# Three gate evictions moved between attention units, and the sink made the initial value of the maximum

## The chip, the cores and the metric

The kernel runs on one core of one Trainium2 chip, as one launch. The metric is the device time of the launch in microseconds (us). The kernel before takes 884.95 us, the median of three runs (884.6 to 885.35). A profiled execution is a run of its own with its own time, so every sum is made against that one and then set beside the median.

## The reference, cut to what matters

Two transformer blocks run over 256 tokens of width 1024, all in float32. The first block has two layers. Its second layer has two attention parts and a gate for each: part c (three branches: selected keys, window keys and 15 compressed keys) with gate z_c, and part d (a window of 128 keys with a learned sink for each head) with gate z_d.

```
def _masked_softmax(s, mask, sink=None):
    s = jnp.where(mask, s, NEG)
    m = jnp.max(s, axis=-1, keepdims=True)
    if sink is not None:
        m = jnp.maximum(m, sink)
    e = jnp.where(mask, jnp.exp(s - m), 0.0)
    den = jnp.sum(e, axis=-1, keepdims=True)
    if sink is not None:
        den = den + jnp.exp(sink - m)
    return e / jnp.maximum(den, TINY)

y_c = _merge_heads(o_c) * jax.nn.silu(z_c)
y_d = _merge_heads(o_d) * jax.nn.silu(z_d)
x = x + concat(y_c, y_d) @ w_out[layer]
```

So for part d the maximum takes the sink in, and the denominator gets exp(sink - maximum) added. d_sinks is one number for each of 8 heads.

## The kernel before, in words

The five engines run five instruction lists written out by hand, and semaphores order them; there is no planner. Nearly all matrix products are split in three (high by high, low by high, high by low), so TensorE has most of the work. ScalarE makes the high parts of the weights, GpSimd the low parts; both also serve other work.

**The stage of the change.** The attention of the second layer is the call `narrow_attention(PART["c"] + PART["d"], FILL_CD)`: 16 units. Units 0 to 11 are part c: for each pair of heads (0, 1) and each half of the queries (0, 1) three branches, where the branches with real keys have 128 or 256 key columns and the third has 15. Units 12 to 15 are part d. A unit holds four heads and passes through these steps:

- `scores(u)` on TensorE, eight small matmuls into two PSUM banks;
- `score_max(u)` on VectorE: scale, bias and maximum. For c with real keys and for d it is four fused operations (L1983, in the trace CUSTOM_DVE_ANT_0 with a DVE_READ_ACCUMULATOR2_ANT behind each) and a short reduction that negates;
- `exps(u)` on ScalarE: four Exp with the negated maximum as bias and the sum as accumulator (L1507);
- `normalise(u)` on VectorE: reciprocal, gate factor, and one wide multiplication (L2043);
- `transposes(u, r)` on TensorE (L990), then `transposed_out(u)` on ScalarE (L1540);
- `mix(step)` on TensorE (L1021) once the last unit of a step is there, and `mixed_out` on VectorE (L2060), which frees the bank for the next mix.

**What is put between.** `FILL_CD` has one list of names for each unit i. TensorE does, at unit i: scores(i+2), transposes(i), the mix of unit i-1 if it ended a step, then the names of the list. A name such as `zc1.0` is half of the product of gate z_c, heads 1 (24 matmuls), `zd0.0.0` a quarter (12). `H:0` and `H:1` are the first quarters of the output product, and they read parts of y whose low half GpSimd makes (L711) from a high half that ScalarE makes (`L:y0`, `L:y1`, L1634).

A name `E:zc1` is the eviction of a gate. It is skipped by TensorE and has two halves. ScalarE does a tanh of the bank (L1550), at unit i ahead of exps(i+1). VectorE then does (tanh + 1) times the bank (L2071) and frees the bank; at unit i this stands behind normalise(i) and ahead of mixed_out and of score_max(i+2). Each engine takes its list in order, so what waits holds all that stands behind it.

**Banks.** Two PSUM banks serve the products of this stage in turn: bank 0 holds zc0, zc1, zd0 and wo1_0 one after the other, bank 1 holds sp_kd, modA, zd1 and wo1_1. So the first matmul of zc1.0 waits for the eviction of zc0, that of zd0.0.0 waits for that of zc1, and H:0 (wo1_0 and wo1_1) waits for those of zd0 and zd1.

**Scaled biases.** Part d needs its bias table scaled; `scale_bias("d", pair, half)` on ScalarE is four copies (L1524), and the dictionaries SCALE_BEFORE and SCALE_BEHIND say at which unit it stands ahead of or behind transposed_out. (0, 0) stands behind transposed_out(2) before the change. The first reader is score_max(12).

**The sink before.** `score_max` of a d unit reduces to `top` in PSUM (L2008), takes the minimum with the negated sinks `no_sinks` (L2014), copies it to the statistics (L2016) and adds the sinks (L2017). ScalarE makes one Exp over the four sums (L1510). `no_sinks` is made once at the start (L2191).

Of the kernel before, what the change touches and what calls it, by code (L numbers as in the profile page):

```python
# [7 lines left out]
ALU = mybir.AluOpType  # L8
ACT = mybir.ActivationFunctionType
AX = mybir.AxisListType  # L10
# [53 lines left out]
    "S: N:kd E:zc0", "zc1.0 E:kd", "zc1.1", "E:zc1", "modA zd0.0.0", "zd0.0.1 E:modA", "",  # L64
    "zd0.1", "zd1.0 E:zd0", "", "zd1.1.0", "zd1.1.1", "L:y0", "H:0 E:zd1 L:y1", "H:1", "")]
SCALE_BEFORE, SCALE_BEHIND = {6: (0, 1), 12: (1, 1)}, {2: (0, 0), 7: (1, 0)}
# [249 lines left out]
def mixer_kernel(nc, a, out):  # L316
    ctx = ExitStack()
    with ctx:
# [14 lines left out]
        def cut(ap, n):  # L333
            return ap.rearrange("p (k n) -> p k n", n=n)
# [57 lines left out]
        stream_rstd, no_sinks = rstd[:, 352:356], rstd[:, 360:368]  # L392
# [165 lines left out]
        def root_of(name):  # L558

            return q_rms[:, "cd".index(name[1]), int(name[2])] if name[0] == "q" else rstd_of(name)  # L560

# [850 lines left out]
        def _(act):  # L1412
# [85 lines left out]
            def exps(u):  # L1498
                part, step, br, last_br, at, qt, n = UNITS[u]
                act.wait_ge(mx_ready, u + 1)  # L1500
                s, e = stat[:, u % 3], prob(u)
                if part == "a":
                    nc.scalar.activation(e[:, 0:AG, 0:n], e[:, 0:AG, 0:n], ACT.Exp, bias=s[:, 4:5],
                                         accum_out=s[:, 8:9]).then_inc(exp_done, 1)
                    return
                for i in range(4):
                    last = nc.scalar.activation(e[:, i, 0:n], e[:, i, 0:n], ACT.Exp, bias=s[:, 4 + i:5 + i],  # L1507
                                                accum_out=s[:, 8 + i:9 + i])
                if part == "d":
                    last = nc.scalar.activation(s[:, 12:16], s[:, 12:16], ACT.Exp)  # L1510
                last.then_inc(exp_done, 1)
# [355 lines left out]
        def _(dve):  # L1867
# [92 lines left out]
            def score_max(u):  # L1960
# [17 lines left out]
                if part == "d" or part == "c" and br:  # L1978
                    dve.wait_ge(sem(f"{part}_bias"), 2 * at + qt + 1)
                    for i in range(4):  # L1980
                        f, bi = divmod(i, 2)
                        i8 = 4 * qt + 2 * bi + f
                        ins = V.tensor_tensor_reduce(out=e[:, i, 0:n], in0=sc[f][:, S * bi:S * bi + n], in1=bias_of(part, at, qt, i),  # L1983
                                                     scale=q_rstd[:, "bcd".index(part), at, i8:i8 + 1], scalar=-3e38,
                                                     op0=ALU.add, op1=ALU.max, accum_out=s[:, 8 + i:9 + i])
                    ins.then_inc(sc_free, 1)
                    dve.wait_ge(sc_free, u + 1)
                    if part == "c":
                        V.tensor_reduce(s[:, 4:8], s[:, 8:12].unsqueeze(2), AX.X, ALU.max, negate=True).then_inc(mx_ready, 1)
                        return  # L1990
# [17 lines left out]
                own.did(V.tensor_reduce(top, e[:, :, 0:n] if part == "c" else s[:, 8:12].unsqueeze(2), AX.X, ALU.max, negate=True))  # L2008
                own.settle()
                if part == "c":  # L2010
                    V.tensor_scalar(s[:, 4:8], top, 1e28, None, ALU.min).then_inc(mx_ready, 1)
                    return
                sk, down = (cut(v[:], 4)[:, :, 2 * at:2 * at + 2] for v in (sinks, no_sinks))
                own.did(V.tensor_tensor(cut(top, 2), cut(top, 2), down, ALU.min))  # L2014
                own.settle()
                own.did(V.tensor_copy(s[:, 4:8], top))  # L2016
                V.tensor_tensor(cut(s[:, 12:16], 2), cut(top, 2), sk, ALU.add).then_inc(mx_ready, 1)  # L2017
# [173 lines left out]
            own.did(V.tensor_scalar(no_sinks, sinks, -1.0, None, ALU.mult))  # L2191
# [475 lines left out]
```

## Time and profile before

| what | value |
|---|---|
| median of the runs shown | 884.95 us (884.6 to 885.35) |
| the profiled execution's own time | 884.18 us |
| its span | 882.4 us |
| TensorE busy | 863.6 us, 98% of the span |
| ScalarE busy | 468.2 us, 53% |
| VectorE busy | 408.9 us, 46% |
| GpSimd busy | 674.2 us, 76% |
| mean granted TensorE clock | 0.996 |
| chain that ended last | TensorE 95%, VectorE 2%, ScalarE 1% |

How to read it: 1.78 us lie around the span in the profiled execution (884.18 less 882.4). A row of the timeline has the start, the length of the merged piece, engine, line and operation, what is written and read, how many instructions, and in brackets the idle time of the engine just before and what released it. An instruction's start can lie ahead of the end of the one before it, since the engines overlap the ends; so the distance between two starts is the price of an instruction in a row of them, and its length that of one that somebody waits for.

### The profile page before, as it was taken

What the parts mean: (1) busy time and instruction counts of PE and PEld (TensorE: products, weight loads), DVE (VectorE), ACT (ScalarE), POOL (GpSimd) and SP (SyncE); (2) the same over time, 40 slices, a digit from 0 to 9 for tenths busy, and PEclk for the clock granted to TensorE, in tenths of its full rate; (3) what the DMA queues carried; (4) which work ended last, traced back from release to release, by engine and by line L of the source; (5) the groups of instructions that cost most, each with busy time, mean ns of one, the idle gap of its engine ahead of it and who ended that gap; (6) DMA issues with size and microseconds to landing.
All of it is one profiled execution on the core that took longest, in us unless ns stands there. A gap on an engine that the chain in (4) does not pass through costs nothing.

```text
span 882.4 us, 17028 instructions
## 1 busy us (share of the span) xinstructions
PE 863.6 (98%) x6944; PEld 817.8 (93%) x6944; DVE 408.9 (46%) x1015; ACT 468.2 (53%) x706; POOL 674.2 (76%) x552
## 2 busy tenths in 40 slices
PE   7999999999989999999999999999999999999997
PEld 6899899998879999889997899999999999999997
DVE  3899745635785576953554223321124642210001
ACT  4545766377876623344444565875336665534431
POOL 0987549748935799798767787678899899987880
PEclk9999999999999999999999999999999999999998
DMA  8855586884210597876575444545546555545521
GB/s 324 339 186 198 204 292 226 307 313 144 87 59 2 205 408 261 344 276 242 195 268 181 166 144 148 188 143 192 191 147 246 191 186 188 189 144 191 192 96 48
DMA packets 28484, 177.62 MB, mean 201 GB/s; under 512 B 3144, under 2 KB 5844, under 8 KB 8056
## 3 DMA queue, kind: packets, MB, share of 16 engines
q1 hardware_dynamic: 27112, 174.87, 54.0%
q10 hardware_dynamic: 1296, 1.68, 0.6%
q8 instruction: 55, 0.90, 0.4%
q14 instruction: 21, 0.17, 0.1%
HBM read 174.95 MB, written 3.43 MB: 202 GB/s over the span
## 4 chain that ended last, share of the span: by engine, by line
PE 95%; DVE 2%; ACT 1%; issue 1%; POOL 1%; DMA 1%; POOLq 0%; SPq 0%; DVEq 0%; ACTq 0%
PE proj L793 20%; PE proj L795 19%; PE proj L796 19%; PE proj L829 4%; PE proj L874 3%; PE proj L872 3%; PE proj L875 3%; PE mixed L1021 1%; PE scores L976 1%; PE transposed L990 1%; PE proj L1074 1%; PE proj L1143 1%; PE mixed L1004 1%; PE scores L963 1%; PE proj L1077 1%; PE proj L1076 1%
## 5 line engine op out<-in xcount | busy, mean ns | idle before, releaser
L695 POOL TENSOR_TENSOR w_lo<-raw,w_hi 128x512 fp32r<-128x512 f32 x348 | 445.2, 1320 | 126.3 <-ACT w_hi L1434 126.3
L795 PE MATMUL proj<-parts,w_lo 128*128 128x256 f32 x1000 | 279.4, 279 | 0.6 <-POOL w_lo L695 0.6
L793 PE MATMUL proj<-parts,w_hi 128*128 128x256 f32 x952 | 270.3, 284 | 0.6 <-POOL w_lo L695 0.4
L796 PE MATMUL proj<-parts,w_hi 128*128 128x256 f32 x952 | 265.8, 279 | 0.0
L1434 ACT ACTIVATE w_hi<-raw 128x2048 fp32r<-128x2048 f32 x84 | 161.0, 1917 | 109.3 <-DMA raw<-in_weights 58.9
L795 PEld LDWEIGHTS proj<-parts,w_lo 128*128 128x128 f32 x1000 | 188.1, 188 | 1.7 <-POOL w_lo L695 0.8
L793 PEld LDWEIGHTS proj<-parts,w_hi 128*128 128x128 f32 x952 | 179.0, 188 | 3.4 <-issue 2.2
L796 PEld LDWEIGHTS proj<-parts,w_hi 128*128 128x128 f32 x952 | 179.0, 188 | 0.0
L695 POOL TENSOR_TENSOR w_lo<-arena,w_hi 128x512 fp32r<-128x512 f32 (+2 forms) x56 | 67.7, 1245 | 27.3 <-ACT w_hi L1434 27.3
L1446 ACT ACTIVATE arena<-proj 128x512 f32<-128x512 f32 x32 | 18.9, 597 | 53.2 <-PE proj L796 36.5
L872 PE MATMUL proj<-w_hi,parts 128*128 128x512 f32 x112 | 45.1, 403 | 0.0
L796 PE MATMUL proj<-hid_lo,w_hi 128*128 128x256 f32 x160 | 44.9, 281 | 0.0
L793 PE MATMUL proj<-hid_hi,w_hi 128*128 128x256 f32 x160 | 44.9, 281 | 0.0
L795 PE MATMUL proj<-hid_hi,w_lo 128*128 128x256 f32 x160 | 44.9, 281 | 0.0
L874 PE MATMUL proj<-w_lo,parts 128*128 128x512 f32 x112 | 44.4, 396 | 0.0
L875 PE MATMUL proj<-w_hi,parts 128*128 128x512 f32 x112 | 44.3, 395 | 0.0
L695 POOL TENSOR_TENSOR w_lo<-raw,w_hi_a 128x512 fp32r<-128x512 f32 x28 | 37.7, 1386 | 4.1 <-ACT w_hi_a L1434 4.1
L2518 DVE SCALAR_TENSOR_TENSOR xT<-proj,mod,xT 128x256 f32<-128x256 f32 x8 | 3.9, 484 | 79.1 <-PE proj L796 79.1
L695 POOL TENSOR_TENSOR w_lo<-raw,w_hi_b 128x512 fp32r<-128x512 f32 x20 | 26.4, 1369 | 9.5 <-ACT w_hi_b L1434 9.4
L2538 DVE SCALAR_TENSOR_TENSOR scores<-proj,tmp 128x512 f32<-128x512 f32 x14 | 9.8, 699 | 44.0 <-ACT tmp L1842 44.0
L793 PEld LDWEIGHTS proj<-hid_hi,w_hi 128*128 128x128 f32 x160 | 30.2, 188 | 0.0
L796 PEld LDWEIGHTS proj<-hid_lo,w_hi 128*128 128x128 f32 x160 | 30.1, 188 | 0.0
(448 smaller groups left out, 2157.0 us busy)
## 6 DMA issues: line engine op xcount, KB each, us to landing
raw<-in_weights SPq DMA_DIRECT2D x106, 1024.0 KB, 5.0
arena<-in_weights SPq DMA_DIRECT2D x31, 1024.0 KB, 7.6
wide<-in_weights SPq DMA_DIRECT2D x9, 1024.0 KB, 6.9
probT<-in_weights SPq DMA_DIRECT2D x8, 1024.0 KB, 5.0
dil_lines<-dil_line SPq DMA_DIRECT2D x1, 2304.0 KB, 12.3
prob<-in_weights SPq DMA_DIRECT2D x2, 1024.0 KB, 4.8
dil_bias<-dil_lines SPq DMA_DIRECT2D x1, 1536.0 KB, 9.8
xT<-in_x SPq DMA_DIRECT2D x4, 256.0 KB, 5.6
```

Source lines behind the costliest of these rows:

```text
L695: nc.gpsimd.tensor_tensor(lo_slots[RAW_AT[n]][:, at], raw_slots[RAW_AT[n]][:, at], hi_slots[HI_AT[m]][:, at].bitcast(F32), ALU.subtract).t ...
L793: nc.tensor.matmul(dst, whi, h, start=first, stop=False)
L795: nc.tensor.matmul(dst, wlo, h, start=False, stop=False)
L796: last = nc.tensor.matmul(dst, whi, lo[:, k, :], start=False, stop=stop)
L829: last = nc.tensor.matmul(pair["banks"][i][:, S * j:S * j + S], w[low][:, k, P * j:P * j + P], parts[:, part, k, :], start=fresh, stop=fin ...
L872: nc.tensor.matmul(banks[t], parts[:, 0, kk, at], whi[:, k, :], start=kk == 0, stop=False)
L874: nc.tensor.matmul(banks[t], parts[:, 0, kk, at], wlo[:, k, :], start=False, stop=False)
L875: last = nc.tensor.matmul(banks[t], parts[:, 1, kk, at], whi[:, k, :], start=False, stop=kk == KD - 1)
L963: last = nc.tensor.matmul(sc[g // 2][:, S * (g % 2):S * (g % 2) + n], q, akT[:, g, S * at:S * at + n], start=True, stop=True)
L1434: nc.scalar.activation(hi_slots[HI_AT[m]][:, 0:kt * w], raw_slots[RAW_AT[n]][:, 0:kt * w], ACT.Copy) \
L1446: nc.scalar.activation(dst, b[:], fn, scale=scale).then_inc(free_of(name), 1)
L2538: V.scalar_tensor_tensor(square, bank(name)[:], 0.0, r, ALU.max, ALU.mult).then_inc(free_of(name), 1)
```

## The change

The evictions of zc0, zc1 and zd1 move to other units: zc0 from unit 0 to 1, zc1 from 3 to 4, zd1 from 13 to 12. The scaled bias (0, 0) moves from behind transposed_out(2) to behind transposed_out(3). In the d units the sink is the `scalar` of the fused operation, that is the value the maximum starts from; the three short operations and the sums behind them go, and ScalarE makes exp(sink - maximum) as four Exp of one column with the sink column as input and the negated maximum as bias, where there was one Exp of four columns. `no_sinks` goes.

```
 FILL_CD = [x.split() for x in (
-    "S: N:kd E:zc0", "zc1.0 E:kd", "zc1.1", "E:zc1", "modA zd0.0.0", "zd0.0.1 E:modA", "",
-    "zd0.1", "zd1.0 E:zd0", "", "zd1.1.0", "zd1.1.1", "L:y0", "H:0 E:zd1 L:y1", "H:1", "")]
-SCALE_BEFORE, SCALE_BEHIND = {6: (0, 1), 12: (1, 1)}, {2: (0, 0), 7: (1, 0)}
+    "S: N:kd", "zc1.0 E:zc0 E:kd", "zc1.1", "", "E:zc1 modA zd0.0.0", "zd0.0.1 E:modA", "",
+    "zd0.1", "zd1.0 E:zd0", "", "zd1.1.0", "zd1.1.1", "E:zd1 L:y0", "H:0 L:y1", "H:1", "")]
+SCALE_BEFORE, SCALE_BEHIND = {6: (0, 1), 12: (1, 1)}, {3: (0, 0), 7: (1, 0)}
...
-        stream_rstd, no_sinks = rstd[:, 352:356], rstd[:, 360:368]
+        stream_rstd = rstd[:, 352:356]
...
+        def sink_of(at, i):
+
+            f, b = divmod(i, 2)
+            return sinks[:, 2 * at + b + 4 * f:][:, 0:1]
...
-                if part == "d":
-                    last = nc.scalar.activation(s[:, 12:16], s[:, 12:16], ACT.Exp)
+                for i in range(4) if part == "d" else ():
+                    last = nc.scalar.activation(s[:, 12 + i:13 + i], sink_of(at, i), ACT.Exp, bias=s[:, 4 + i:5 + i])
...
                         ins = V.tensor_tensor_reduce(out=e[:, i, 0:n], in0=sc[f][:, S * bi:S * bi + n], in1=bias_of(part, at, qt, i),
-                                                     scale=q_rstd[:, "bcd".index(part), at, i8:i8 + 1], scalar=-3e38,
+                                                     scale=q_rstd[:, "bcd".index(part), at, i8:i8 + 1],
+                                                     scalar=sink_of(at, i) if part == "d" else -3e38,
                                                      op0=ALU.add, op1=ALU.max, accum_out=s[:, 8 + i:9 + i])
...
-                    if part == "c":
-                        V.tensor_reduce(s[:, 4:8], s[:, 8:12].unsqueeze(2), AX.X, ALU.max, negate=True).then_inc(mx_ready, 1)
-                        return
+                    V.tensor_reduce(s[:, 4:8], s[:, 8:12].unsqueeze(2), AX.X, ALU.max, negate=True).then_inc(mx_ready, 1)
+                    return
...
-                sk, down = (cut(v[:], 4)[:, :, 2 * at:2 * at + 2] for v in (sinks, no_sinks))
-                own.did(V.tensor_tensor(cut(top, 2), cut(top, 2), down, ALU.min))
-                own.settle()
-                own.did(V.tensor_copy(s[:, 4:8], top))
-                V.tensor_tensor(cut(s[:, 12:16], 2), cut(top, 2), sk, ALU.add).then_inc(mx_ready, 1)
+                V.tensor_scalar(s[:, 4:8], top, 1e28, None, ALU.min).then_inc(mx_ready, 1)
...
-            own.did(V.tensor_scalar(no_sinks, sinks, -1.0, None, ALU.mult))
```

## Rows read from the trace of the kernel before

**Rows 1.** The page: its first line, span and number of instructions.
```profile
span 882.4 us, 17028 instructions
```

**Rows 2.** Busy time by stretch: stretch, length, PE, PEld, DVE, ACT, POOL, clock, DMA, GB/s.
```profile
203.00:272.00 69.00, 64.60 (x639) 56.81 (x637) 49.83 (x220) 51.10 (x181) 50.76 (x54) 1.00 0.21 73
...
874.00:876.00 2.00, 0.83 (x5) 0.75 (x6) 0.27 (x2) 1.08 (x3) 0.00 (x0) 0.95 0.00 0
```

**Rows 3.** Timeline of TensorE, units 0 to 6 of the stage.
```profile
210.26 0.62 PE L976 MATMUL scores<-arena 64*128 64x15 f32 x8
...
213.82 0.37 PE L1074 MATMUL proj<-parts,w_hi 128*128 128x256 f32 x1
...
225.63 0.66 PE L990 MATMUL proj<-cols,wide 128*128 128x128 f32 x4 [0.66 <-DVE wide L2043]
...
226.70 0.36 PE L1074 MATMUL proj<-parts,w_hi 128*128 128x256 f32 x1
...
231.59 0.66 PE L990 MATMUL transposed<-cols,prob 128*128 128x128 f32 x4
```

**Rows 4.** Timeline of VectorE over the same units.
```profile
210.56 0.69 DVE L2071 SCALAR_TENSOR_TENSOR arena<-arena,proj 128x512 f32<-128x512 f32 x1 [1.27 <-ACT arena L1550]
211.17 0.65 DVE L1996 SCALAR_TENSOR_TENSOR prob<-scores,q_rstd,cmp_bias 128x15 f32<-128x15 f32 x4
...
212.67 0.69 DVE L2043 TENSOR_TENSOR wide<-wide,sums 128x512 f32<-128x512 f32 x1
...
221.96 0.69 DVE L2071 SCALAR_TENSOR_TENSOR arena<-arena,proj 128x512 f32<-128x512 f32 x1 [0.51 <-ACT arena L1550]
...
225.49 0.42 DVE L2060 SCALAR_TENSOR_TENSOR arena<-mixed,arena 128x256 f32<-128x256 f32 x1
225.82 0.34 DVE L1983 CUSTOM_DVE_ANT_0 prob<-scores,dil_bias,q_rstd 128x128 f32<-128x128 f32 x1
...
230.85 0.69 DVE L2043 TENSOR_TENSOR prob<-prob,sums 128x512 f32<-128x512 f32 x1
```

**Rows 5.** Timeline of ScalarE, units 2 to 4.
```profile
219.01 1.27 ACT L1524 ACTIVATE dil_bias<-arena,q_rms 128x128 f32<-128x128 f32 x4
221.32 0.60 ACT L1550 ACTIVATE arena<-proj 128x512 f32<-128x512 f32 x1 [1.04 <-PE proj L1077]
...
224.92 0.59 ACT L1540 ACTIVATE probT<-transposed 128x512 f32<-128x512 f32 x1
225.40 0.31 ACT L1507 ACTIVATE prob<-prob,stat 128x15 f32<-128x15 f32 x1
```

**Rows 6.** Timeline of VectorE: end of the maximum of a c unit, then a d unit.
```profile
219.62 0.09 DVE L1983 DVE_READ_ACCUMULATOR2_ANT stat<- 128x1 f32 x1
219.74 0.16 DVE L1989 TENSOR_REDUCE stat<-stat 128x4 f32<-128x4 f32 x1
...
252.57 0.08 DVE L1983 DVE_READ_ACCUMULATOR2_ANT stat<- 128x1 f32 x1
...
253.26 0.15 DVE L2017 TENSOR_TENSOR stat<-sums,cols 128x4 f32<-128x4 f32 x1
```

**Rows 7.** Timeline of ScalarE, unit 12.
```profile
255.44 0.19 ACT L1510 ACTIVATE stat<-stat 128x4 f32<-128x4 f32 x1
255.53 1.70 ACT L1524 ACTIVATE arena<-arena,q_rms 128x256 f32<-128x256 f32 x4
257.79 0.60 ACT L1540 ACTIVATE probT<-transposed 128x512 f32<-128x512 f32 x1 [0.55 <-PE mixed L1021]
```

**Rows 8.** Timeline of TensorE, units 12 and 13.
```profile
254.69 0.66 PE L990 MATMUL transposed<-cols,prob 128*128 128x128 f32 x4 [1.18 <-DVE prob L2043]
...
260.60 0.66 PE L1021 MATMUL mixed<-probT,arena 128*64 128x128 f32 x8 [0.83 <-DVE arena L2060]
261.18 0.38 PE L829 MATMUL proj<-parts,w_hi_b 128*128 128x256 f32 x1
```

**Rows 9.** Timeline of GpSimd, the low part that H:0 reads.
```profile
258.98 1.27 POOL L711 TENSOR_TENSOR parts<-arena,parts 128x512 fp32r<-128x512 f32 x1 [11.43 <-ACT parts L1634]
```

More of the change, by code:

```diff
@@ L2007, in score_max @@
                 top = st[:, S + 12 + 4 * (u % 3):S + 12 + 4 * (u % 3) + 4]
-                own.did(V.tensor_reduce(top, e[:, :, 0:n] if part == "c" else s[:, 8:12].unsqueeze(2), AX.X, ALU.max, negate=True))
+                own.did(V.tensor_reduce(top, e[:, :, 0:n], AX.X, ALU.max, negate=True))
                 own.settle()
-                if part == "c":
-                    V.tensor_scalar(s[:, 4:8], top, 1e28, None, ALU.min).then_inc(mx_ready, 1)
-                    return
-                sk, down = (cut(v[:], 4)[:, :, 2 * at:2 * at + 2] for v in (sinks, no_sinks))
-                own.did(V.tensor_tensor(cut(top, 2), cut(top, 2), down, ALU.min))
-                own.settle()
-                own.did(V.tensor_copy(s[:, 4:8], top))
-                V.tensor_tensor(cut(s[:, 12:16], 2), cut(top, 2), sk, ALU.add).then_inc(mx_ready, 1)
+                V.tensor_scalar(s[:, 4:8], top, 1e28, None, ALU.min).then_inc(mx_ready, 1)
             def normalise(u):
```

## The prediction

> **What bounds the kernel now.** I read the page first: a span of 882.4 us [rows 1], in which TensorE is the engine of nearly the whole chain. A change that adds and takes no TensorE work can then only move the stretches in which TensorE stands still. The second view is the busy time by stretch. In the stage of the change, from 203 to 272 us, TensorE is busy 64.60 of 69.00 us at a granted clock of 1.00, and no other engine is near that [rows 2]. So 4.4 us of standing still is all that is at stake in the stage. The third view is the timeline of each engine through the 16 units; there one looks for the bracket behind a TensorE row. The larger brackets are 0.66 us ahead of transposes(4) [rows 3], 1.18 us ahead of transposes(12) and 0.83 us ahead of the mix of unit 12 [rows 8]. They name VectorE, whose list in turn waits for ScalarE. What TensorE loses or gains here stays to the end, since behind the stage each engine's work starts from TensorE's products again.
>
> **The sink.** Its work is off TensorE, but it lies in the path score, maximum, Exp, normalise, transpose. On VectorE the distance from the start of the last accumulator read to the end of the maximum is 0.84 us in a d unit (252.57 to 253.26 + 0.15) and 0.28 us in a c unit, which already has the new form (219.62 to 219.74 + 0.16) [rows 6]. So each d unit gives back 0.56 us. The pointer as initial value has no row: the fused operation of a c unit has one pointer already. The nearest thing is an accumulator read, 0.08 us [rows 6]; the bounds are 0 and four times that, 0.32 us a unit, and I take 0, as the number of instructions stays. On ScalarE one Exp of four columns becomes four of one column. The one in the trace lasts 0.19 us, but the next starts 0.09 us behind it [rows 7]. Three more cost 3 x 0.09 = 0.27 us if they overlap likewise, 3 x 0.19 = 0.57 us if not. I take 0.27, the row of starts. The net is 0.29 us off the path of each d unit; TensorE sees it only where it waits for it. The negated sinks at the start are one small VectorE operation while TensorE has a first product in hand; nothing.
>
> Here the Trainium skill speaks against the change. ScalarE: Activation LUTs, "Rules for kernel authors", budgets about 0.3 us for every ACTIVATE with a pointer as bias; three more would be an estimate of 0.9 us, more than the 0.56 us saved. The row of starts here disagrees with it for a short operation.
>
> **zc0, from unit 0 to unit 1.** Before, VectorE waited 1.27 us for the tanh, and the eviction then stood ahead of the maximum of unit 2, which started at 211.17 [rows 4]. Its scores were done at 210.26 + 0.62 = 210.88 [rows 3], so it now starts some 0.06 later, 0.23 us earlier than before. Normalise(1) follows it, its wide multiplication at 212.67 - 0.23 = 212.44; the eviction starts 0.61 behind (the distance of the rows at 210.56 and 211.17 is that of one 512-wide operation) at 213.05 and ends at 213.74 [rows 4]. The product zc1.0 must wait for it, and the shortest handover in the rows is 0.05 (wide operation ending at 230.85 + 0.69 = 231.54, transposes at 231.59 [rows 3, 4]); for a product whose weights are loaded behind the wait I estimate 0.1 to 0.15. That is 213.9 against 213.82 [rows 3]: **0.1 us lost** in place of nothing won. The tanh itself is hidden in ScalarE's idle time.
>
> **zc1, from unit 3 to unit 4, with the scaled bias.** This is the large term. ScalarE's list at unit 3 is now exps(4), transposed_out(3), the four copies of the bias, and only then, at unit 4, the tanh of zc1. transposed_out(3) can't come earlier: it waits for TensorE's mix. Its second half starts at 224.92 and what follows at 225.40 [rows 5]. The copies take 1.27 us less the 0.09 of overlap, 1.2 [rows 5, 7]. So the tanh starts at 226.6 and ends at 227.2, with 0.1 us from zc0 at 227.3, where it started at 221.32 before [rows 5]. zd0.0.0 needs the bank of zc1: the eviction takes 0.69 us [rows 4], so it ends at about 228.0 and the product starts at 228.1, not at 226.70 [rows 3]. **Here TensorE stands still for some 1.9 us**, in place of 0.66. It doesn't end there: the eviction holds VectorE's list, in which mixed_out and the maximum of unit 6 stand behind it. From the eviction's start at 227.3 the maximum of unit 6 begins 0.61 + 0.33 later (distances of starts [rows 4]), at 228.2, against 225.82 before: 2.4 us later. From there VectorE has no idle time in the trace up to normalise(6), whose wide operation started at 230.85 and ended at 231.54, and transposes(6) start at 231.59 [rows 3, 4]. All of that moves by the 2.4. So the cost is **2.4 us** from transposes(6) on (1.4 at zd0.0.0, the rest as new waits for the maximum of unit 7 and for normalise(6)), the 0.1 of zc0 within it. The 0.66 us before transposes(4) do shrink, but what they give is spent at zd0.0.0. Between units 7 and 11 I find nothing that gives any of it back: the waits there are TensorE on its own results, and they move with it.
>
> The old place of the copies cost nothing: at 219.01 they lay in ScalarE's idle time ahead of the tanh, which shows 1.04 us of idle behind them [rows 5].
>
> **zd1, from unit 13 to unit 12, with the sink.** Transposes(12) waited 1.18 us for normalise(12) [rows 8]; it comes 0.56 earlier by the shorter maximum, and the eviction stands behind it. Gain 0.56. The mix of unit 12 waited 0.83 us for mixed_out(11), which stood behind the eviction of zd1, itself late by the tanh. With the eviction gone from there mixed_out(11) waits for its mix alone, and the 0.83 go. Next is H:0, which needs the low part from GpSimd. That started at 258.98 and lasted 1.27 [rows 9], 0.93 us ahead of H:0 at 261.18 [rows 8]. It hangs on transposed_out(12) at 257.79, which had 0.55 us of idle ahead [rows 7]. That work now ends a little later (the tanh of zd1 eats what the shorter maximum gives exps(13), and the sink adds 0.27), so the copy can move forward by only 0.4, and H:0 can start at 258.98 - 0.4 + 1.27 + 0.1 = 259.95, by 1.2 earlier. The two gains sum to 1.39, this bound says 1.23; in between, **1.3 us gained**. In units 14 and 15 the path has slack, and the waits stay.
>
> **Sum.** 2.4 - 1.3 = +1.1 us. The profiled execution took 884.18 us, so 885.3 for one like it; it stands 0.77 below the median of 884.95, so the median to expect is 884.95 + 1.1 = **886.1**. With the unseen costs at their upper ends the ScalarE path to H:0 is 0.3 longer (+1.4); the pointer at its bound gives +1.3; both act on that one point and don't add up fully. Sizes of the handovers, about 0.1 each over five of them, are good for 0.3 either way. The likeliest case alone: 885.4 to 886.8.
>
> **The rivals.**
> A. The gains come and the loss doesn't: the copies of the bias slip in ahead of transposed_out(3), where ScalarE now has to wait for the mix, or zd0 doesn't wait. That gives -1.3 + 0.1 = -1.2, 883.8. For it: with the tanh gone from unit 3, exps(4) is done earlier and leaves such a gap, and TensorE had 0.66 us to give at unit 4. Against: each list is kept in order, and the copies are written behind a step that waits for the mix. 0.07.
> B. The short Exp run at full price, 0.19 each or more. Place: ScalarE between exps(13) and transposed_out(12), from there the low part and H:0. It decides once ScalarE ends later than the mix, which it does from the first tenth on. By rows +1.4, 886.4. 0.14. By the estimate from the Trainium skill above it would be about +1.8, 886.7.
> C. Slower clearly: TensorE's clock falls. At the end of the kernel it is busy 0.83 of 2.00 us and the granted clock goes to 0.95 and below [rows 2]. The new stall at 226 to 228 is alike in size, with two shorter ones after it. If the clock went to half (1.2 in place of 2.4 GHz) for 2 to 3 us of products, those would take twice as long: +2 to +3 more, 888 to 889. For: the sum of standing still from 225 to 234 is about 3 us. Against: the stage has waits of 1.18 us now at 1.00. 0.09. The Trainium skill (TensorE: Matmul & The Clock Gate, "What's actually happening") has the same two states and says that activity releases the throttle; the trace agrees at the kernel's end.
>
> **Chances.** Forecast 0.70, A 0.07, B 0.14, C 0.09. A measurement of this kernel can tell about 0.2%, 1.8 us, from no change: faster is below 883.2, slower above 886.7. Faster needs A with luck: 0.03. Slower is C, a third of B and a part of the forecast's upper end: 0.22. The same: 0.75. The range leaves out A and C: 884.5 to 887.2.
>
> **What would show it.** TensorE's first matmul of zd0 with a bracket of nearly 2 us, released by VectorE L2071 (its line after the change); new brackets before scores(8) and transposes(6); ScalarE's bias copies at about 225.5; the bracket before transposes(12) about 0.6 and none before the mix of unit 12; a short one before H:0 that names GpSimd. Wrong: no bracket at zd0 (A), starts 0.2 us apart in the four short Exp (B), a clock below 1.00 near 230 (C), or a gain in units 7 to 11 that takes up the delay.

## The result, and the profile after

The kernel after takes 886.5 us (median of 21 runs, 885.02 to 887.7), the kernel before beside it on the same chip 884.95 (21 runs, 883.67 to 886.66). The ratio is 1.0016 with a 95% interval of 1.001 to 1.0022, that is 0.9 to 1.9 us slower. The forecast was 886.1, 1.1 us slower, which lies in that interval. The profiled execution took 885.45 us, its span is 883.7 against 882.4 [rows 1].

The page of the kernel after, its first line and the busy time of each engine:

```profile
span 883.7 us, 17024 instructions
...
PE 863.9 (98%) x6944; PEld 817.5 (93%) x6944; DVE 408.2 (46%) x1002; ACT 469.7 (53%) x718; POOL 674.0 (76%) x552
```

TensorE is busy 863.9 us against 863.6 and its work is unchanged, so at least 1.0 of the 1.3 us is time in which it stands still. Busy time by stretch (columns as in [rows 2]): the stage, the stretch of the new wait, and the end of the kernel, then that end in the kernel before:

```profile
203.00:272.00 69.00, 64.43 (x628) 56.48 (x627) 48.51 (x209) 52.92 (x192) 49.17 (x54) 1.00 0.22 76
226.00:230.00 4.00, 2.48 (x22) 2.28 (x20) 2.22 (x12) 3.83 (x16) 4.00 (x7) 1.00 0.02 6
876.00:878.00 2.00, 1.05 (x8) 0.97 (x9) 0.18 (x1) 0.99 (x3) 0.00 (x0) 1.00 0.00 0
```

```profile
876.00:878.00 2.00, 1.85 (x8) 1.55 (x8) 0.97 (x2) 0.11 (x1) 0.00 (x0) 0.50 0.00 0
```

**How long the stage is.** Where the stage starts moves from profile to profile with what happened ahead of it (mostly by tenths of a microsecond, by 2 and 4 us in two runs below), so I compare lengths, not positions: from the start of transposes(0) to the start of the mix of unit 15. Before, that is 209.73 to 270.90, 61.17 us; after, 210.31 to 272.74, 62.43 us: **+1.26**. A second profile of the kernel after gives 62.44, so tenths, and nearly hundredths, mean something here, while a median of whole runs tells only about 1 us. The difference of the two spans is the start of the stage (+0.58), the stage (+1.26) and what is behind it (-0.54). The last is the very end: before, the granted clock from 876 to 878 us was 0.50, after it was 1.00, and the last two groups of four matmuls start 0.54 us apart instead of 1.02. The change has no work there, and over the profiles of this study the clock in these last microseconds is 1.00 in some and 0.50 in others; by what, I didn't study.

TensorE's timeline of the kernel after, all rows of the stage that the argument needs (in brackets the idle time before the row and what ended it):

```profile
210.31 0.60 PE L995 MATMUL transposed<-cols,prob 128*128 128x128 f32 x4
...
225.72 0.63 PE L995 MATMUL proj<-cols,wide 128*128 128x128 f32 x4 [0.20 <-ACT probT L1545]
...
228.48 0.39 PE L1079 MATMUL proj<-parts,w_hi 128*128 128x256 f32 x1 [1.52 <-DVE arena L2069]
...
233.32 0.62 PE L981 MATMUL scores<-arena 64*128 64x15 f32 x8 [0.46 <-DVE stat L1988]
234.44 0.66 PE L995 MATMUL transposed<-cols,prob 128*128 128x128 f32 x4 [0.50 <-DVE prob L2041]
...
255.89 0.71 PE L981 MATMUL scores<-arena 64*128 64x128 f32 x8 [0.20 <-DVE stat L1988]
257.21 0.66 PE L995 MATMUL transposed<-cols,prob 128*128 128x128 f32 x4 [0.60 <-DVE prob L2041]
...
262.21 0.66 PE L1026 MATMUL mixed<-probT,arena 128*64 128x128 f32 x8
263.12 0.36 PE L834 MATMUL proj<-parts,w_hi_b 128*128 128x256 f32 x1 [0.25 <-POOL parts L716]
...
272.74 1.09 PE L1026 MATMUL mixed<-probT,arena 128*64 128x128 f32 x16 [0.63 <-DVE scores L2058]
```

Read it in two halves. Up to transposes(6) TensorE loses. The first matmul of zd0.0.0 now waits 1.52 us, and scores(8) and transposes(6) wait 0.46 and 0.50 where they waited for nothing; only transposes(4) wait less, 0.20 instead of 0.66. Transposes(6) start 24.13 us into the stage (234.44 less 210.31), before 21.86 (231.59 less 209.73 [rows 3]): +2.27. From there to the last mix TensorE gains: 38.30 us against 39.31, -1.01. Transposes(12) wait 0.60 instead of 1.18, the mix of unit 12 has no bracket where it had 0.83 [rows 8], and there are two new short ones, 0.20 before scores(14) and 0.25 before H:0. 2.27 - 1.01 = 1.26.

VectorE and ScalarE around the first half:

```profile
227.74 0.69 DVE L2069 SCALAR_TENSOR_TENSOR arena<-arena,proj 128x512 f32<-128x512 f32 x1 [2.58 <-ACT arena L1555]
228.35 0.42 DVE L2058 SCALAR_TENSOR_TENSOR arena<-mixed,arena 128x256 f32<-128x256 f32 x1
228.68 0.34 DVE L1988 CUSTOM_DVE_ANT_0 prob<-scores,dil_bias,q_rstd 128x128 f32<-128x128 f32 x1
```

```profile
225.48 0.59 ACT L1545 ACTIVATE probT<-transposed 128x512 f32<-128x512 f32 x1
225.95 1.27 ACT L1529 ACTIVATE dil_bias<-arena,q_rms 128x128 f32<-128x128 f32 x4
227.12 0.59 ACT L1555 ACTIVATE arena<-proj 128x512 f32<-128x512 f32 x1
```

This is one chain: transposed_out(3), the four bias copies, the tanh of zc1, the eviction on VectorE, and then two who wait for it. TensorE waits for the bank, and VectorE's own list has mixed_out and the maximum of unit 6 behind the eviction, while VectorE was idle for 2.58 us ahead of it. And around the second half, ScalarE, then GpSimd:

```profile
258.18 0.84 ACT L1515 ACTIVATE stat<-cols,stat 128x1 f32<-128x1 f32 x4
258.92 1.69 ACT L1529 ACTIVATE arena<-arena,q_rms 128x256 f32<-128x256 f32 x4
260.52 0.58 ACT L1545 ACTIVATE probT<-transposed 128x512 f32<-128x512 f32 x1
```

```profile
261.70 1.28 POOL L716 TENSOR_TENSOR parts<-arena,parts 128x512 fp32r<-128x512 f32 x1 [12.47 <-ACT parts L1639]
```

### The profile page after: what moved, and what is told of

The parts are those of the page before. It is cut to its first block, busy times and chain, and to the rows that moved or that the text cites. A ratio compares the mean times of both kernels' runs of the same rounds, so it can differ in the third digit from the quotient of the medians.

```text
span 883.7 us, 17024 instructions
## 1 busy us (share of the span) xinstructions
PE 863.9 (98%) x6944; PEld 817.5 (93%) x6944; DVE 408.2 (46%) x1002; ACT 469.7 (53%) x718; POOL 674.0 (76%) x552
## 4 chain that ended last, share of the span: by engine, by line
PE 95%; ACT 2%; DVE 1%; POOL 1%; issue 1%; DMA 0%; POOLq 0%; SPq 0%; DVEq 0%; ACTq 0%
PE proj L798 20%; PE proj L800 19%; PE proj L801 19%; PE proj L834 4%; PE proj L879 3%; PE proj L877 3%; PE proj L880 3%; PE mixed L1026 1%; PE scores L981 1%; PE transposed L995 1%; PE proj L1079 1%; PE proj L1148 1%; PE proj L1081 1%; PE proj L1082 1%; PE mixed L1009 1%; PE scores L968 1%
## 5 line engine op out<-in xcount | busy, mean ns | idle before, releaser
L1491 ACT ACTIVATE wide<-xT 128x256 f32<-128x256 f32 (+1 forms) x11 | 5.3, 494 | 47.2 <-DVE xT L2515 44.2
```

## The experiments

Every kernel here computes the whole function. The measure is the stage's length in the profile; where there is a ratio it is that of whole runs against the kernel before on the same chip.

| kernel | stage, us | against before | median, us | before beside it | ratio (95%) |
|---|---|---|---|---|---|
| before | 61.17 | | 884.95 | | |
| after | 62.43 | +1.26 | 886.5 | 884.95 | 1.0016 (1.001 to 1.0022) |
| after, second profile | 62.44 | +1.27 | 885.53 (one) | 884.65 | |
| sink only | 60.76 | -0.41 | 884.03 | 885.02 | 0.9995 (0.9979 to 1.0011) |
| zc1 and copies only | 63.47 | +2.30 | 887.26 | 885.02 | 1.0024 (1.0016 to 1.0033) |
| after, copies back | 61.28 | +0.11 | 884.94 | 885.02 | 0.9996 (0.998 to 1.0011) |
| after, zc1 and copies back | 60.12 | -1.05 | 883.83 | 885.02 | 0.9987 (0.9979 to 0.9996) |
| zd1 only | 60.44 | -0.73 | 883.82 | 884.8 | 0.9989 (0.998 to 0.9998) |
| after, eviction of zc1 last in VectorE's unit | 61.45 | +0.28 | 885.02 | 884.8 | 1.0007 (0.9998 to 1.0016) |
| after, zd0.0.0 one unit later | 65.04 | +3.87 | 888.04 | 884.8 | 1.0034 (1.0021 to 1.0048) |
| one Exp, sum by VectorE | 60.14 | -1.03 | 883.48 | 884.8 | 0.9986 (0.9977 to 0.9995) |
| copies only | 61.95 | +0.78 | 886.9 (one) | 884.65 | |
| zc1 only | 62.30 | +1.13 | 885.62 (one) | 884.65 | |
| one Exp, sum by GpSimd | 59.94 | -1.23 | 883.8 | 884.65 | 0.9986 (0.9977 to 0.9995) |

My theory: the loss and the gain are two separate sums, +2.4 from the order of ScalarE's list at unit 3 and 4, and -1.3 from the d units. The rivals: that the loss belongs to something else (the sink's pointer, zc0), that it is one single wait and not two, and that the four short Exp eat the sink's gain.

### The sink alone

The kernel after with the lists of before:

```
-    "S: N:kd", "zc1.0 E:zc0 E:kd", "zc1.1", "", "E:zc1 modA zd0.0.0", "zd0.0.1 E:modA", "",
-    "zd0.1", "zd1.0 E:zd0", "", "zd1.1.0", "zd1.1.1", "E:zd1 L:y0", "H:0 L:y1", "H:1", "")]
-SCALE_BEFORE, SCALE_BEHIND = {6: (0, 1), 12: (1, 1)}, {3: (0, 0), 7: (1, 0)}
+    "S: N:kd E:zc0", "zc1.0 E:kd", "zc1.1", "E:zc1", "modA zd0.0.0", "zd0.0.1 E:modA", "",
+    "zd0.1", "zd1.0 E:zd0", "", "zd1.1.0", "zd1.1.1", "L:y0", "H:0 E:zd1 L:y1", "H:1", "")]
+SCALE_BEFORE, SCALE_BEHIND = {6: (0, 1), 12: (1, 1)}, {2: (0, 0), 7: (1, 0)}
```

> The sink part alone: all evictions and the scaled bias stay where they were. The stage is measured from the start of transposes(0) to the start of the last mix: 61.17 us before, 62.43 after. Theory (the move of zc1 with the bias copies makes the loss): 60.6 to 61.0, that is 0.2 to 0.6 shorter; in the after trace the maximum of a d unit is 0.3 us shorter but the four short Exp take 0.65 more, so the net on the path of one unit can be above zero and only the wait before transposes(12) shrinks. Rival (the sink's short Exp and its second pointer are the loss): 62 or more. Time: theory 884.4 to 884.8, rival 886 or more.

Its stage is 60.76 us, -0.41. TensorE's timeline, units 12 and 13:

```profile
253.77 0.72 PE L981 MATMUL scores<-arena 64*128 64x128 f32 x8 [0.20 <-DVE stat L1988]
255.09 0.66 PE L995 MATMUL transposed<-cols,prob 128*128 128x128 f32 x4 [0.60 <-DVE prob L2041]
...
261.00 0.66 PE L1026 MATMUL mixed<-probT,arena 128*64 128x128 f32 x8 [0.82 <-DVE arena L2058]
```

The wait before transposes(12) falls by 0.58 (the row distance of [rows 6] had said 0.56), the mix of unit 12 keeps its wait (0.82), and a new 0.20 stands before scores(14): 0.58 - 0.20 = 0.38 of the 0.41. So the sink alone gains, and the loss isn't its. The whole runs can't tell it from no change.

### The eviction of zc1 and the copies alone

The kernel before with these two moves and nothing else:

```
-    "S: N:kd E:zc0", "zc1.0 E:kd", "zc1.1", "E:zc1", "modA zd0.0.0", "zd0.0.1 E:modA", "",
+    "S: N:kd E:zc0", "zc1.0 E:kd", "zc1.1", "", "E:zc1 modA zd0.0.0", "zd0.0.1 E:modA", "",
-SCALE_BEFORE, SCALE_BEHIND = {6: (0, 1), 12: (1, 1)}, {2: (0, 0), 7: (1, 0)}
+SCALE_BEFORE, SCALE_BEHIND = {6: (0, 1), 12: (1, 1)}, {3: (0, 0), 7: (1, 0)}
```

> The kernel before with two edits only: the eviction of zc1 at unit 4 and the bias copies (0, 0) behind unit 3. Theory: 2.3 us longer in the stage (63.5), with a wait of 1.9 at the first matmul of zd0, 0.5 before scores(8), 0.6 before transposes(6), and the waits of 1.2 and 0.8 at units 12 and 13 as before; time 887.2. Rival (the sink is the loss): the stage within 0.3 of 61.2, time 885.

63.47 us, +2.30, and the time confirms it: 1.0024. TensorE's timeline:

```profile
228.38 0.39 PE L1074 MATMUL proj<-parts,w_hi 128*128 128x256 f32 x1 [1.53 <-DVE arena L2071]
...
233.21 0.62 PE L976 MATMUL scores<-arena 64*128 64x15 f32 x8 [0.46 <-DVE stat L1983]
234.33 0.66 PE L990 MATMUL transposed<-cols,prob 128*128 128x128 f32 x4 [0.50 <-DVE prob L2043]
...
257.43 0.66 PE L990 MATMUL transposed<-cols,prob 128*128 128x128 f32 x4 [1.18 <-DVE prob L2043]
...
263.33 0.66 PE L1021 MATMUL mixed<-probT,arena 128*64 128x128 f32 x8 [0.82 <-DVE arena L2060]
```

The first three brackets are those of the kernel after to a hundredth, the last two those of the kernel before. The whole loss of the change is here, and it reaches the end of the stage undiminished.

### Each of the two by itself

First the kernel after with the copies back behind unit 2 (`SCALE_BEHIND` 3 to 2), then with the eviction of zc1 back at unit 3 as well:

```
-SCALE_BEFORE, SCALE_BEHIND = {6: (0, 1), 12: (1, 1)}, {3: (0, 0), 7: (1, 0)}
+SCALE_BEFORE, SCALE_BEHIND = {6: (0, 1), 12: (1, 1)}, {2: (0, 0), 7: (1, 0)}
```

> The changed kernel with the bias copies (0, 0) back behind unit 2. Theory: the tanh of zc1 starts 1.2 earlier, so the wait at zd0 falls to about 0.7 and the stage to 61.3 (0.1 to 0.3 above before); time 885.1 to 885.4. Rival (the copies are hidden, the place of the eviction behind normalise(4) makes the loss by itself): the stage stays at 62.2 or more, time 886.3.

```
-    "S: N:kd", "zc1.0 E:zc0 E:kd", "zc1.1", "", "E:zc1 modA zd0.0.0", "zd0.0.1 E:modA", "",
+    "S: N:kd", "zc1.0 E:zc0 E:kd", "zc1.1", "E:zc1", "modA zd0.0.0", "zd0.0.1 E:modA", "",
```

> The changed kernel with zc1 back at unit 3 and the bias copies behind unit 2; zc0, zd1 and the sink stay changed. Theory: 0.8 us shorter than before in the stage (60.4), time 884.2. Rival (zc0's move or the sink costs more than its 0.1 or its gain): at or above 61.2, time 885.

61.28 and 60.12 us; the second is 0.3 below what I had expected for it. So in the kernel after the copies cost 62.43 - 61.28 = 1.15, and the eviction's own move 61.28 - 60.12 = 1.16. With the copies back TensorE's timeline reads:

```profile
227.38 0.38 PE L1079 MATMUL proj<-parts,w_hi 128*128 128x256 f32 x1 [0.38 <-DVE arena L2069]
...
232.22 0.62 PE L981 MATMUL scores<-arena 64*128 64x15 f32 x8 [0.47 <-DVE stat L1988]
233.34 0.66 PE L995 MATMUL transposed<-cols,prob 128*128 128x128 f32 x4 [0.50 <-DVE prob L2041]
```

The copies are paid where TensorE waits for the bank, 1.52 against 0.38, and nowhere else. The two waits behind it are those of the eviction's place. Two runs add the moves one at a time to the kernel before instead; each edit is one of the two lines above:

> The kernel before with the bias copies (0, 0) behind unit 3 and nothing else. Theory (ScalarE's list at unit 4 is 1.2 us later, so Exp and transposed copies of units 5 and 6 are late): 0.8 us longer in the stage (61.95), shown as waits before scores(8) and transposes(6). Rival (the copies alone are hidden and only the tanh behind them counts): 61.17 within 0.1.

> The kernel before with the eviction of zc1 at unit 4 and nothing else. Theory: 1.1 us longer in the stage (62.3), the difference that the changed kernel with the copies back showed against the one with zc1 back as well (61.28 less 60.12 = 1.16): the wait of 0.66 before transposes(4) falls to 0.2, 0.4 at zd0, 0.5 before scores(8), 0.5 before transposes(6). Rival: the move alone is hidden, 61.2.

The copies alone give +0.78, zc1 alone +1.13. (The one whole run of the copies alone, 886.9, is late for another reason: its stage starts at 211.94, 2.2 us after that of the kernel before. More on this at the clock below.) So the eviction's move costs the same with and without the rest of the change (1.13 and 1.16). The copies cost 1.15 or 1.17 behind a moved eviction (62.43 - 61.28; 63.47 - 62.30), but 0.78 without it, by another way. TensorE's timeline of the copies alone:

```profile
233.47 0.62 PE L976 MATMUL scores<-arena 64*128 64x15 f32 x8 [0.33 <-DVE stat L1983]
234.59 0.66 PE L990 MATMUL transposed<-cols,prob 128*128 128x128 f32 x4 [0.50 <-DVE prob L2043]
```

There is no wait at zd0.0.0, since the tanh is long done; what the copies delay is the Exp of unit 5 behind them on ScalarE, and through it VectorE and TensorE. Alone the two moves sum to 1.91, together they cost 2.30.

### The eviction put last in VectorE's unit

This splits the other cost, VectorE's held list, from the bank. Everything as in the kernel after, but VectorE evicts zc1 behind mixed_out and the maximum of unit 6:

```
                     for name in prompt(fill[i]):
-                        between(name)
+                        if name != "zc1":
+                            between(name)
                     if i >= 2 and UNITS[units[i - 2]][3]:
                         mixed_out(units[i - 2])
                     if i + 2 < len(units):
                         score_max(units[i + 2])
+                    if "zc1" in prompt(fill[i]):
+                        between("zc1")
```

> The changed kernel, with the eviction of zc1 on VectorE behind mixed_out and the maximum of unit 6, at the same unit 4; TensorE and ScalarE lists stay. It tells the two halves of the loss apart. Theory (the eviction's wait for the tanh holds VectorE's list, and the maxima of units 6 and 7 behind it): the wait of about 1.5 at zd0 stays, those before scores(8) and transposes(6) go, and the stage falls by about 1.0 from 62.4 to 61.4. Rival (only the bank of zc1 holds TensorE, and the two later waits come from the mod columns): 62.3 or more.

61.45 us, 0.98 less than after. TensorE's timeline, all brackets behind transposes(4) and up to unit 10:

```profile
228.56 0.38 PE L1079 MATMUL proj<-parts,w_hi 128*128 128x256 f32 x1 [1.53 <-DVE arena L2069]
...
249.25 0.63 PE L995 MATMUL proj<-cols,wide 128*128 128x128 f32 x4 [0.20 <-ACT probT L1545]
```

The bank wait is as long as in the kernel after (1.53), and the brackets before scores(8) and transposes(6) are gone. 0.46 + 0.50 = 0.96: **the held list costs 1.0 us**, and what remains, 61.45 - 60.12 = 1.33 against the kernel with zc1 and the copies back, is the bank. In the kernel after VectorE is idle for 2.58 us in front of that eviction, to 227.74, and the scores for the maximum behind it are done at 225.52 (224.81 + 0.71). In whole runs this is 1.0007 against 1.0016, and these two intervals overlap: the 0.98 are shown by the profile alone.

### The bank's reader moved away as well

The mirror image: VectorE's order as in the kernel after, but zd0.0.0, the reader of the bank, in unit 5:

```
-    "S: N:kd", "zc1.0 E:zc0 E:kd", "zc1.1", "", "E:zc1 modA zd0.0.0", "zd0.0.1 E:modA", "",
+    "S: N:kd", "zc1.0 E:zc0 E:kd", "zc1.1", "", "E:zc1 modA", "zd0.0.0 zd0.0.1 E:modA", "",
```

> The changed kernel with the first quarter of zd0 at unit 5 in place of 4, so that no product waits for the bank of zc1 at unit 4. If the bank alone were the trouble (rival) the stage would fall to 61.2 or less. Theory (VectorE's list is held as well, so scores(7) wait for the maximum of unit 6): TensorE waits at scores(7) in place of zd0, 3 us in one piece, and the stage is 0.5 longer than that of the changed kernel, 62.9.

Here I was wrong: 65.04 us, not 62.9, and 1.0034 in whole runs. TensorE's timeline and its windows over the same time:

```profile
230.21 1.23 PE L981 MATMUL scores<-arena 64*128 64x128 f32 x8 [3.04 <-DVE stat L1988]
...
232.41 0.41 PE L1081 MATMUL proj<-parts,w_lo 128*128 128x256 f32 x1
232.62 0.41 PE L1082 MATMUL proj<-parts,w_hi 128*128 128x256 f32 x1
...
236.51 0.27 PE L1082 MATMUL proj<-parts,w_hi 128*128 128x256 f32 x1
```

```profile
226.00:230.00 4.00, 1.17 (x10) 1.02 (x10) 2.04 (x10) 4.00 (x16) 4.00 (x6) 0.87 0.06 23
230.00:234.00 4.00, 3.79 (x21) 3.41 (x22) 3.48 (x25) 2.66 (x12) 4.00 (x5) 0.50 0.01 4
234.00:238.00 4.00, 4.00 (x31) 3.67 (x32) 1.22 (x5) 2.87 (x12) 4.00 (x6) 0.78 0.00 0
```

Without the product the next thing in TensorE's list is scores(7), which needs the banks that VectorE's maximum of unit 6 frees, and that stands behind the eviction: TensorE stands still for 3.04 us in one piece, where the kernel after waits 1.52 and then fills the rest with the twelve matmuls of zd0.0.0. During that wait the granted clock goes from 1.00 to 0.50, 1.2 in place of 2.4 GHz: behind it the products of 256 columns start 0.21 us apart instead of 0.12, the eight score matmuls take 1.23 instead of 0.71, and 1.00 is back only near 236 us. From scores(7) to the last of the 24 products behind it TensorE takes 6.30 us (230.21 to 236.51); at 1.00, in the kernel before, the same steps take 1.01 (scores(7) to the first product, 228.29 to 229.30) and 2.78 (24 products, 213.82 to 216.60), in all 3.79. The low clock costs 2.5 us here, and that covers the 2.1 us over my expectation. So rival C of the prediction is a real mechanism, but the kernel after, with 1.52, 0.46 and 0.50 within 8 us, shows 1.00 throughout. The Trainium skill (TensorE: Matmul & The Clock Gate, "What's actually happening") has these two states and lets activity release the lower one; the trace agrees.

That the wait has to be so long isn't shown. In the profile of the copies alone TensorE waited 0.44 us for ScalarE ahead of the stage, and the clock fell some 2 us later:

```profile
191.48 0.63 PE L1278 MATMUL proj<-probT,small 128*128 128x30 f32 x4 [0.44 <-ACT probT L1737]
```

```profile
194.00:195.00 1.00, 1.00 (x7) 1.00 (x6) 0.00 (x0) 0.91 (x3) 0.00 (x0) 0.50 1.04 434
```

It was back at 197 us. In the kernels before and after, the same product has no bracket and the clock stays at 1.00 from 188 to 200 us. So a wait of 0.44 us was followed by 0.50 there, while 1.52, 0.46 and 0.50 us in the stage of the kernel after were not: what decides it stays open.

### zd1 alone

```
-    "zd0.1", "zd1.0 E:zd0", "", "zd1.1.0", "zd1.1.1", "L:y0", "H:0 E:zd1 L:y1", "H:1", "")]
+    "zd0.1", "zd1.0 E:zd0", "", "zd1.1.0", "zd1.1.1", "E:zd1 L:y0", "H:0 L:y1", "H:1", "")]
```

> The kernel before with one edit: the eviction of zd1 at unit 12 in place of 13. Theory: the wait of 0.83 before the mix of unit 12 goes and nothing else changes; the stage is 60.6 in place of 61.17, time 884.4. Rival (the eviction now holds the maximum of unit 14 and delays ScalarE): within 0.2 of 61.17.

60.44 us, -0.73: the 0.83 before the mix of unit 12 are gone, the 1.18 before transposes(12) stay. I had expected 60.6. With the sink's -0.41 that makes -1.14; the kernel after with zc1 and the copies back, which has both and the move of zc0, shows -1.05.

### One Exp instead of four

To price the four short Exp I kept the sink as the initial value, had VectorE make the four sums behind the maximum's signal (so ScalarE's first Exp doesn't wait for it), and ScalarE one Exp over four columns. The lists are zd1 at 12, all else as before:

```
-                for i in range(4) if part == "d" else ():
-                    last = nc.scalar.activation(s[:, 12 + i:13 + i], sink_of(at, i), ACT.Exp, bias=s[:, 4 + i:5 + i])
+                if part == "d":
+                    act.wait_ge(sem("sink_sum"), u - PART["d"][0] + 1)
+                    last = nc.scalar.activation(s[:, 12:16], s[:, 12:16], ACT.Exp)
...
                     V.tensor_reduce(s[:, 4:8], s[:, 8:12].unsqueeze(2), AX.X, ALU.max, negate=True).then_inc(mx_ready, 1)
+                    if part == "d":
+                        dve.wait_ge(mx_ready, u + 1)
+                        V.tensor_tensor(cut(s[:, 12:16], 2), cut(s[:, 4:8], 2), cut(sinks[:], 4)[:, :, 2 * at:2 * at + 2], ALU.add) \
+                            .then_inc(sem("sink_sum"), 1)
                     return
```

> What the measured prices point to: zd1 at unit 12, zc0, zc1 and the bias copies where they were; the sink as initial value of the maximum, but sink - maximum made by one VectorE operation that nobody on the path waits for, and one Exp of four columns as before. Theory: 1.1 to 1.3 us shorter in the stage than before (60.0), and no longer than e4 (60.12); time 883.7. Rival (the short Exp are hidden, so that only the order counts): the same as e4 within 0.1.

60.14 us, as long as the 60.12 of the kernel with four Exp, zc1 and the copies back. That is the number that I had given the rival (the short Exp are hidden), but not for its reason. Two sides cancel: the wait before H:0 (0.25) is gone, and the sum on VectorE takes 0.21 from what the sink had won before transposes(12), 0.81 instead of 0.60:

```profile
254.51 0.66 PE L995 MATMUL transposed<-cols,prob 128*128 128x128 f32 x4 [0.81 <-DVE prob L2046]
```

The last run gives the sum to GpSimd, ahead of its low parts, in the kernel after with zc1 and the copies back (the sum as above, in GpSimd's list behind its own wait for the maximum):

> e4 (zc0 and zd1 moved, zc1 and the copies where they were, sink as initial value) with one Exp of four columns, its input, sink less maximum, made by GpSimd, which stands idle in these units. Against e8, where VectorE made it: the wait before transposes(12) should be 0.60 as in e4 and not 0.81, and the 0.25 before H:0 should be gone as in e8. Theory: a stage of 59.9, 0.2 shorter than e4 and e8 (60.12, 60.14), time 883.5. Rival (the small GpSimd operation or its handover is slow and ScalarE waits for it): 60.2 or more.

```profile
258.10 0.20 POOL L717 TENSOR_TENSOR stat<-stat,cols 128x4 f32<-128x4 f32 x1 [4.08 <-DVE stat L2003]
```

```profile
259.29 0.66 PE L1003 MATMUL transposed<-cols,prob 128*128 128x128 f32 x4 [0.60 <-DVE prob L2050]
```

```profile
260.27 0.19 ACT L1524 ACTIVATE stat<-stat 128x4 f32<-128x4 f32 x1
...
262.39 0.60 ACT L1554 ACTIVATE probT<-transposed 128x512 f32<-128x512 f32 x1 [0.34 <-PE mixed L1034]
```

59.94 us: 0.60 before transposes(12) and no bracket before H:0. (This profile reached its stage 4.4 us later than that of the kernel after, at 214.72: TensorE had waited 0.68 and 1.29 us for ScalarE near 192 and 194 us, and the granted clock was 0.57 from 196 to 200. In the stage itself it is 1.00.) Against the same kernel with four Exp (60.12) that is 0.18 less, and so much the four short Exp cost in this kernel. This kernel and the one with the sum on VectorE have the same ratio, 0.9986 (0.9977 to 0.9995): both are faster than the kernel before and the kernel after; between them the runs don't decide.

The kernel after once more, for what a profile repeats to:

> The changed kernel once more, to see how far the length of the stage repeats from one profiled execution to another. Every theory: 62.43 within 0.1, while the start of the stage may move by some tenths with the first load.

62.44 against 62.43 us.

## Why the prediction was right

**zc0: the step held, its last term was a little high.** The eviction started 3.31 us into the stage, forecast 213.05 less 209.73 = 3.32. It ended at 214.30 and zc1.0 started at 214.36: a handover of 0.06, where I had taken 0.1 to 0.15. So zc1.0 starts at 4.05 in the stage against 4.09 before [rows 3]: nothing lost in place of 0.1. The nearest row had 0.05, I had set the estimate above it, and the row was right.

**zc1 and the copies: right, in each step.** Forecast were the copies at about 225.5, the tanh at 226.6 to 226.7, a wait of nearly 2 us at zd0.0.0 and 2.4 us at transposes(6). The stage began 0.58 later in this profile; with that taken off, the copies started at 225.37, the tanh at 226.54, zd0.0.0 at 227.90 (forecast 228.1), and transposes(6) came 2.27 later than before. By starts the product is 1.20 late (18.17 into the stage, before 16.97), forecast 1.4; the missing 0.2 are the 0.1 of zc0 and the 0.05 to 0.1 of the handover, neither of which came. The bracket is 1.52, forecast 1.9: transposes(4) start 0.49 earlier in the stage (15.41, before 15.90), which makes 1.69 with the 1.20, and the last 0.17 lie under the end of the matmul before, where no bracket counts them. The 2.4 didn't hang on the bracket. That two costs are in it, the bank and VectorE's held list, was argued from the order of the lists; the run with the eviction last shows it, 0.98 for the list. Nothing between units 7 and 11 gave any of it back: the run with zc1 and the copies alone keeps +2.30 to the end.

**zd1 and the sink: right mechanism, gain 0.3 too high.** Forecast -1.3, measured -1.01. The two large terms came as forecast: 0.56 at transposes(12) (0.58 measured), and the whole 0.83 at the mix of unit 12. H:0 waits for GpSimd, as forecast, 0.25. What was mis-sized are the two costs without a row:

- The pointer as initial value. I took 0, with a bound of 0.32 us a unit. The groups of the fused operation in the kernel after, by shape (number, then least, mean and most ns):

```profile
L1988 DVE CUSTOM_DVE_ANT_0 prob<-scores,dil_bias,q_rstd x8: 342/347/351, 204.0 to 229.5; 128x128 f32<-128x128 f32 x8
L1988 DVE CUSTOM_DVE_ANT_0 prob<-scores,dil_bias,cols x8: 405/407/409, 250.1 to 258.7; 128x128 f32<-128x128 f32 x8
```

  With the sink column it takes 407 ns instead of 347, 60 more, four times a unit: 0.24 us, inside the bound and far from the 0 I took. It shows as the new 0.20 before scores(14), in every kernel that has the sink as a pointer, and by starts: from transposes(6) to transposes(12) TensorE takes 22.77 us where it took 23.10 (254.69 less 231.59 [rows 3, 8]), so it gains 0.33, the 0.56 less the 0.24. "The number of instructions stays" was no reason.
- The four short Exp. Their group in the kernel after:

```profile
L1515 ACT ACTIVATE stat<-cols,stat x16: 280/291/302, 254.1 to 267.8; 128x1 f32<-128x1 f32 x16
```

  Each takes 0.29 us and the four 0.84; the next instruction starts 0.74 behind the first (258.18 to 258.92), where it was 0.09 [rows 7]. That is 0.65 more a unit, above my upper bound of 0.57: the one Exp that I priced them by has no pointer as its bias, and I took it for the same instruction. Rival B's mechanism is therefore what happened. Its price in the end is small, 0.18 (four Exp against one with the sum on GpSimd), because there was slack for most of it: transposed_out(12) had 0.55 us of idle time ahead of it [rows 7], which the four Exp use up (no bracket at 260.52), and with one Exp 0.34 of it is back (262.39 in the last run). What is left shows as the 0.25 before H:0, where the forecast's bound had 0.16 (1.39 less 1.23).

  The two close the account: at H:0 TensorE has gained 0.91 (29.59 us from transposes(6) before, 28.68 after) against the bound of 1.23, and 0.24 and 0.09 are missing. Another 0.10 comes behind H:0, which makes the 1.01.

The Trainium skill had the right number, in another section than the one that I weighed. ScalarE: Activation LUTs, "What ACT_TABLE_LOAD costs", gives an ACTIVATE with a [128,1] pointer as bias about 280 ns and 93 ns less without, and lets neighbours overlap by 93 ns. As an estimate from that page four of them start 0.187 apart and the next follows 0.75 behind the first. The trace agrees (0.29 long, 0.74), and the 0.19 and 0.09 of [rows 7] are the same page's values without a pointer. The prediction set its row against the rule and went with the row, but the row was of the other form.

**The sum.** 2.27 - 1.01 = 1.26 for a forecast of 2.4 - 1.3 = 1.1. The loss was forecast 0.13 too high and the gain 0.29 too high, and the two errors partly cancel; that the sum is only 0.16 off is in part luck. The time alone doesn't decide between the forecast (+1.1, 886.1) and rival B (+1.4, 886.4) either: 886.5 is nearer to B. Rival A (no loss) fell with the bracket at zd0.0.0, rival C (the clock) with 1.00 in every stretch of the stage. One name was wrong: the eviction's line after the change is L2069, not L2071.

**What zc0 costs.** The move of zc0 was not run alone, but the profiles tell it, since the sink and zd1 act only from unit 12 on. Transposes(6) start 21.86 us into the stage before, with the sink alone and with zd1 alone, and 21.81 in the kernel with zc1 and the copies back, which has zc0 moved. So the move gains some 0.05 us, in place of the 0.1 lost of the forecast. The sink and zd1 alone sum to -0.41 - 0.73 = -1.14, the kernel that has both and zc0's move shows -1.05: the two don't add by some 0.1, where H:0 waits 0.25 us only if both are there.

## What to carry to other kernels

An eviction that comes late costs twice, at the bank's next user and in its own engine's list: ask what stands behind it, and if that has its inputs already, put it first (here that gave back 1.0 of the 2.3 us). Price an instruction by a row of its own form, pointer operands included; a row of the same operation with a constant in that place isn't its price. And work that fills a wait is worth more than its place in the list suggests: a product taken out of the gap made a wait of 3 us in one piece, and the clock fell on top of it.

## What the runs showed of the hardware

- A second pointer operand on VectorE's fused multiply, add and maximum costs 60 ns an instruction: 347 to 407 ns for 128 columns; for 256 columns the rows are 0.48 before and 0.54 after.
- A short Exp with a pointer as bias is 0.29 us long, and four in a row start 0.185 us apart; a four-column Exp without one is 0.19 us, and the next starts 0.09 behind it.
- Behind a wait of TensorE of 3.04 us it worked at a granted clock of 0.50 for about 5.6 us, which cost some 2.5 us; waits of 1.52, 0.46 and 0.50 within 8 us left it at 1.00; and in one profile the clock was 0.50 from 194 to 197 us behind a wait of only 0.44. The length of the wait alone doesn't decide.
- By its row in the profile GpSimd adds 128x4 in 0.20 us when its list is free, VectorE in 0.16.
